# Expert loop of a routed mixture: row gather and scatter-add by DMA replaced by register-addressed column copies and adds on a transposed residual

## The chip, the cores and the metric

One core of a Trainium2 chip runs the whole program in one launch. The metric is device time in microseconds (us), the median of three runs: 1949.67 us before the change (1949.06 to 1951.79). All data is fp32.

## The reference

Two layers work on 640 tokens of width 1024: 128 context tokens and 512 latent tokens. Each layer does a modulated RMSNorm, one input projection, a convolution module beside differential attention, an output projection with a gated residual, and then a mixture of 16 experts. Each expert picks 80 tokens itself (16 context, 64 latent) by the top affinities, so a token can be picked by several experts or by none:

```python
aff = jax.nn.softmax(jnp.einsum('btd,de->bte', h, w_router).astype(jnp.float32), axis=-1)
gsel, idx = lax.top_k(aff.transpose(0, 2, 1), C)
xs = jax.vmap(lambda hb, ib: hb[ib])(h, idx)
hid = jax.nn.silu(jnp.einsum('becd,edf->becf', xs, w_gate)) * jnp.einsum('becd,edf->becf', xs, w_up)
ye = jnp.einsum('becf,efd->becd', hid, w_down) * gsel[..., None].astype(h.dtype)
return jax.vmap(lambda yb, ib: jnp.zeros((T, D), yb.dtype).at[ib.reshape(-1)].add(yb.reshape(-1, D)))(ye, idx)
...
x = x + g2 * expert_choice(h2, w_router, w_gate, w_up, w_down)
```

`h2` is the normed and modulated residual. A final RMSNorm of both token sets is the output.

## The kernel before

Weights stream through `weight_ring`, six slots of 2 MB. An expert has six units in order: gate (first half of the input features), up (first half), gate and up (second halves), down (two halves). SyncE issues the load of unit i of expert e as soon as unit i of expert e-1 has been used (`expert_used`), so the ring holds one whole expert and the order of the loads is fixed. Weights are the stationary operand; the 80 tokens of an expert are 80 moving columns, in two column groups of the array.

Before the loop, the router phase takes one token tile of 128 after another. For each it forms the residual `x2` (token rows in `x_tile`, stored to `x_res` in DRAM), squares it, gets 1/rms on GpSimd, scales the rows (`x_norm`), stores them to `x_unit` in DRAM, transposes them, modulates them (`h2_t`) and gets the router's logits. VectorE then finds the 8 largest of each expert ten times over (L1364 to L1369). The indices are transposed into `row_idx`, one expert per column.

In the loop, for expert e:

- GpSimd gathers 80 rows of `x_unit` by an indirect DMA (L1546), TensorE transposes them (L746) while expert e-1 is still at work, and VectorE scales and shifts them into `picked_t` (L1418, L1420).
- TensorE does gate and up (L760), ScalarE a SiLU of each half (L1031), VectorE the product (L1426), TensorE down (L777).
- ScalarE copies the result out of PSUM (L1039), TensorE transposes it back to token rows (L790), VectorE applies affinity and gate (L1433), and GpSimd adds the rows into `x_res` by an indirect DMA with addition (L1564).

The order on TensorE is gate and up of e, transposes of the picks of e+1, down of e, transposes of the result of e. It is written out by hand. TensorE, ScalarE and VectorE go round a real loop.

After the loop, all rows of `x_res` are loaded again (`x_all`), squared, scaled and transposed (L486) for the next layer's projection (L527), or squared and scaled for the output (L1456).

## Time and profile before

| | |
|---|---|
| runs of the kernel (3) | 1949.06, 1949.67, 1951.79 us; median 1949.67 |
| the profiled execution | span 1948.8 us from first to last instruction; no other time is given for it |
| mean granted clock of TensorE | 0.952 |
| TensorE matmuls busy | 1717.8 us (88%) |
| VectorE, ScalarE, GpSimd busy | 630.2, 327.0, 139.3 us |
| read from and written to DRAM | 509.30 and 24.64 MB |
| expert loop of layer 0, first gate matmul to last down matmul | 449.68 to 971.75 us |
| expert loop of layer 1 | 1396.28 to 1918.02 us |

The profile shows the busy share of each engine, the transfers, and for each idle time what ended it. A busy share says little about the bound: what counts in the loop is which wait of TensorE ends last. The clock is given as a share of 2.4 GHz, so 0.50 is the lower level of 1.2 GHz.

### The profile page before, as it was taken

To read this page: it belongs to the slowest core of one execution; us is meant where nothing else is said; L and a number is where in the kernel's file an instruction comes from. 1 tells how busy PE (TensorE), PEld (TensorE's weight loads), DVE (VectorE), ACT (ScalarE), POOL (GpSimd) and SP (SyncE) were. 2 spreads that over 40 slices of the span, in tenths; PEclk is the share of its full clock that TensorE was granted. 3 is DMA by queue.
4 is the path that set the end of the run, shared out by engine and by line. 5 is a ranking of instruction groups with operands and counts; after the bars stand their busy time and mean duration, and the time that the engine had idled before them with its cause. 6 is when DMAs were issued, how large, how long until landed. Compare 5 with 4: busy or idle time off the path is not lost.

```text
span 1948.8 us, 60484 instructions
## 1 busy us (share of the span) xinstructions
PE 1717.8 (88%) x28403; PEld 1357.9 (70%) x28403; DVE 630.2 (32%) x1056; ACT 327.0 (17%) x667; POOL 139.3 (7%) x169
## 2 busy tenths in 40 slices
PE   4999988967998899898969998899499999898983
PEld 2555456547998889888845444755489988898883
DVE  2399277251111111010127975832411111010112
ACT  3100156320010101010030003542110101010001
POOL 2100000100000000000010000000000000000002
PEclk9999999988999999999979999999699999999997
DMA  9246540436999999999941643033499999999995
GB/s 360 84 173 236 196 162 1 170 143 239 384 388 399 388 398 399 388 399 387 394 161 55 221 167 139 13 119 130 147 386 389 393 395 399 387 400 389 399 388 211
DMA packets 154439, 534.70 MB, mean 274 GB/s; under 512 B 5937, under 2 KB 6354, under 8 KB 154386
## 3 DMA queue, kind: packets, MB, share of 16 engines
q1 hardware_dynamic: 139600, 484.99, 64.6%
q0 software_dynamic: 12320, 42.47, 7.5%
q10 hardware_dynamic: 2466, 6.50, 0.8%
q8 instruction: 37, 0.61, 0.1%
q14 instruction: 16, 0.13, 0.0%
HBM read 509.30 MB, written 24.64 MB: 274 GB/s over the span
## 4 chain that ended last, share of the span: by engine, by line
PE 57%; DMA 30%; DVE 8%; SPq 2%; ACT 2%; issue 1%; POOL 0%; ACTq 0%; POOLq 0%; DVEq 0%
DMA weight_ring<-in_w_gate_dram 24%; PE ps L760 17%; PE ps L527 14%; PE ps L666 7%; PE ps L777 6%; PE ps L564 3%; DMA weight_ring<-in_w_down_dram 3%; PE ps L457 2%; DVE neg_m L1264 2%; SPq L356 2%; PE ps L626 1%; DMA weight_ring<-in_conv_w_dram 1%; PE ps L790 1%; DVE weight_ring L1300 1%; PE ps L686 1%
## 5 line engine op out<-in xcount | busy, mean ns | idle before, releaser
L760 PE MATMUL ps<-v_sb,weight_ring 128*64 128x80 f32 x16384 | 614.0, 238 | 74.9 <-DMA weight_ring<-in_w_gate_dram 51.4
L760 PEld LDWEIGHTS ps<-v_sb,weight_ring 128*64 128x64 f32 x16384 | 599.1, 141 | 93.0 <-DMA weight_ring<-in_w_gate_dram 54.7
L777 PE MATMUL ps<-mix,weight_ring 128*64 128x80 f32 x8192 | 294.3, 233 | 7.5 <-DMA weight_ring<-in_w_down_dram 4.3
L777 PEld LDWEIGHTS ps<-mix,weight_ring 128*64 128x64 f32 x8192 | 286.5, 137 | 14.5 <-issue 10.1
L527 PE MATMUL ps<-mix,weight_ring 128*128 128x512 f32 (+1 forms) x1024 | 285.1, 439 | 1.3 <-DVE mix L1158 1.0
L527 PEld LDWEIGHTS ps<-mix,weight_ring 128*128 128x128 f32 x1024 | 155.1, 193 | 130.1 <-issue 128.8
L1426 DVE TENSOR_TENSOR mix<-mix,ps 128x320 f32<-128x320 f32 x64 | 28.3, 483 | 644.5 <-PE ps L760 644.5
L1186 DVE SCALAR_TENSOR_TENSOR weight_ring<-u_gate,conv_cols,weight_ring 128x655 f32<-128x655 f32 x240 | 195.3, 887 | 0.0
L666 PE MATMUL ps<-weight_ring,mix 128*128 128x512 f32 x320 | 140.2, 592 | 0.0
L1433 DVE SCALAR_TENSOR_TENSOR qk<-ps,gsel,gate 80x1024 f32<-80x1024 f32 x32 | 41.0, 1280 | 284.7 <-PE ps L790 284.7
L1564 POOL DMA_INDIRECT x_res<-qk,row_idx x32 | 46.2, 1444 | 972.2 <-DVE qk L1433 941.2
L1031 ACT ACTIVATE mix<-ps 128x320 f32<-128x320 f32 x64 | 24.5, 435 | 536.6 <-PE ps L760 536.6
L666 PEld LDWEIGHTS ps<-weight_ring,mix 128*128 128x128 f32 x320 | 59.5, 190 | 67.9 <-issue 67.8
L1039 ACT ACTIVATE mix<-ps 128x320 f32<-128x320 f32 x64 | 28.0, 437 | 446.9 <-PE ps L777 446.9
L564 PE MATMUL ps<-weight_ring,mix 128*128 128x512 f32 x160 | 70.5, 595 | 0.0
L951 ACT ACTIVATE weight_ring<-ps,neg_m 128x640 f32<-128x640 f32 (+1 forms) x80 | 55.7, 706 | 5.1 <-DVE neg_m L1264 5.1
L1264 DVE TENSOR_REDUCE neg_m<-ps 128x2 f32<-128x1280 f32 (+1 forms) x40 | 50.8, 1273 | 15.6 <-PE ps L601 15.3
L564 PEld LDWEIGHTS ps<-weight_ring,mix 128*128 128x128 f32 x160 | 29.7, 190 | 36.4 <-issue 36.4
L457 PE MATMUL ps<-weight_ring,cond_silu 128*32 128x512 f32 x384 | 48.6, 629 | 0.8 <-issue 0.8
L612 PE MATMUL ps<-ident,weight_ring 128*128 128x128 f32 x168 | 32.4, 296 | 18.4 <-DVE o_tok L1283 9.0
L626 PE MATMUL ps<-v_sb,weight_ring 128*128 128x128 f32 x272 | 43.8, 303 | 4.9 <-ACT weight_ring L970 4.8
L626 PEld LDWEIGHTS ps<-v_sb,weight_ring 128*128 128x128 f32 x272 | 35.6, 202 | 10.9 <-ACT weight_ring L970 6.2
(183 smaller groups left out, 1178.0 us busy)
## 6 DMA issues: line engine op xcount, KB each, us to landing
weight_ring<-in_w_gate_dram SPq DMA_DIRECT2D x64, 2048.0 KB, 23.8
weight_ring<-in_w_up_dram SPq DMA_DIRECT2D x64, 2048.0 KB
weight_ring<-in_w_down_dram SPq DMA_DIRECT2D x64, 2048.0 KB, 26.5
weight_ring<-in_w_mod_dram SPq DMA_DIRECT2D x24, 2048.0 KB, 8.2
weight_ring<-in_w_in_dram SPq DMA_DIRECT2D x10, 2048.0 KB, 12.6
weight_ring<-in_w_out_dram SPq DMA_DIRECT2D x4, 2048.0 KB, 9.2
x_res<-x_tile POOLq DMA_DIRECT2D x10, 512.0 KB, 3.3
x_unit<-x_norm ACTq DMA_DIRECT2D x10, 512.0 KB, 2.6
```

Of the source, the lines that this page charges most:

```text
L457: last = nc.tensor.matmul(ps[c * STRIP:(c + 1) * STRIP, 6, :], cond_silu[:, k, at:at + STRIP], w[:, k, :], start=(k < 4 and g == 0), stop= ...
L527: last = nc.tensor.matmul(ps[:, 2 * (n % 3) + bank, 0:cols.stop - cols.start], w[:, k, tokens(b)], mix[:, k, cols], start=(at == 0), stop= ...
L564: last = nc.tensor.matmul(ps[:, 2 * (n % 3), :], mix[:, k, tokens(t)], w[:, k, :], start=(k == 0), stop=(k == KD - 1))
L626: last = nc.tensor.matmul(ps[:, 7, tokens(1)], a_col[:, tokens(j)], vals, start=(j == 0), stop=(j == n - 1))
L666: last = nc.tensor.matmul(ps[:, 2 * (i % 2) + n, :], mix[:, k, tokens(t)], w[:, k % 4, n * BANK:(n + 1) * BANK], start=(at == 0), stop=(at ...
L760: last = nc.tensor.matmul(ps[c * HALF:(c + 1) * HALF, 2 * (i % 2) + f // BLK, f % BLK * CAP:(f % BLK + 1) * CAP], w[:, kk, o:o + HALF], pi ...
L777: last = nc.tensor.matmul(ps[c * HALF:(c + 1) * HALF, 4 + d // BLK, d % BLK * CAP:(d % BLK + 1) * CAP], w[:, kk, o:o + HALF], hid[:, k, :] ...
L951: last = nc.scalar.activation(prob[:, b, m, 0:n], score_rows(s)[:, m, :], ACT.Exp, bias=neg_m[:, b, m:m + 1], accum_out=row_sum[:, b, m:m ...
L1186: ins = nc.vector.scalar_tensor_tensor(acc[:, j, :], src, w, acc[:, j, :], ALU.mult, ALU.add)
L1264: nc.vector.tensor_reduce(neg_m[:, s % 2, :], score_rows(s), AX, ALU.max, negate=True)\
L1433: nc.vector.scalar_tensor_tensor(added, ps[0:CAP, 6:8, :].rearrange("p b n -> p (b n)"), gsel[:, bass.ds(e, 1)], gate2[:], ALU.mult, ALU.m ...
L1564: nc.gpsimd.indirect_dma_start(out=x_res, out_offset=bass.IndirectOffsetOnAxis(ap=row_idx[:, e:e + 1], axis=0), in_=added, in_offset=None, ...
```

## The change

The normed and modulated tokens of all tiles stay on chip, transposed, in `mix`, and the residual stays on chip, transposed, in `x2_t` (features on partitions, one column per token in each of 8 blocks). A picked token is then one column in 8 blocks. Each pick is copied by one instruction whose address comes from a register: GpSimd copies picks 0 to 31 (`pick_lo`), ScalarE picks 32 to 79 (`pick_hi`). The result is added back in the same way: GpSimd adds picks 0 to 31, VectorE picks 32 to 79. The registers are loaded eight at a time. Gather, scatter-add, `x_unit`, `row_idx`, the transposes L746 and L790, the modulation L1418 and L1420 and the copies L1039 go. Affinity times gate is formed on VectorE once per expert (`gain_of`) and multiplied in on the way out of PSUM. In the router phase 1/rms is spread over the partitions by a small matmul. The indices and affinities of all experts go to DRAM and back once per layer. `picked_t` is one buffer, so the picks of e+1 wait for the end of gate and up of e. After the loop TensorE transposes the residual back from `x2_t`. The loops of ScalarE, VectorE and GpSimd are written out; that of TensorE stays a loop.

```diff
+PICK_SPLIT = 32
+PICK_LOAD = 8
...
+        def picks_of(engine, e, at, n):
+            src = top_i[0:1, at:at + n] if e == 0 else pick_row[:, e * CAP + at:e * CAP + at + n]
+            return nc.values_load_multi_w_load_instructions(
+                src, engines=[engine], min_val=0, max_val=(N_LAT if at < CAP_LAT else N_CTX) - 1,
...
+        def picked_row(j, pick):
+            rows = mix[:, :, N_CTX:N_TOK] if j < CAP_LAT else mix[:, :, 0:N_CTX]
+            return rows[:, :, bass.ds(pick, 1)]
...
 # TensorE, after and before the loop
+            def transpose_back(l, t):
+                if t == 0:
+                    pe.wait_ge(*added_lo.at(l - 1, EXPERTS))
+                    pe.wait_ge(*added_hi.at(l - 1, EXPERTS))
+                if t >= 3:
+                    pe.wait_ge(*(x_kept if l < DEPTH else y_ready).at(0, t - 2))
+                for k in range(KD):
+                    last = nc.tensor.transpose(ps[:, 2 * (t % 3) + k // 4, tokens(k % 4)], x2_t[:, k, tokens(t)], ident[:])
...
                 def gate_up(e):
-                    pe.wait_ge(*picked_ready.at(l, e + 1))
+                    pe.wait_ge(*picked_lo_ready.at(l, e + 1))
+                    pe.wait_ge(*picked_hi_ready.at(l, e + 1))
...
                     gate_up(e)
                     pe.wait_ge(*result_taken.at(l, e + 1))
-                    picked_transposes(e + 1)
                     down(e)
-                    result_transposes(e)
...
 # ScalarE
+                def pick_hi(e):
+                    for at in range(PICK_SPLIT, CAP, PICK_LOAD):
...
+                        for j, pick in enumerate(picks_of(mybir.EngineType.Activation, e, at, PICK_LOAD), at):
+                            last = nc.scalar.activation(picked_t[:, :, j:j + 1], picked_row(j, pick), ACT.Copy)
+                    last.then_inc(picked_hi_ready.sem, 1)
...
+                    if e + 1 < EXPERTS:
+                        act.wait_ge(*expert_used.at(l, e * 6 + 4))
+                        pick_hi(e + 1)
...
 # VectorE
+                def keep_x(t):
+                    dve.wait_ge(*x_transposed.at(l, t + 1))
+                    nc.vector.tensor_copy(x_stage[t], ps[:, 2 * (t % 3):2 * (t % 3) + 2, :].rearrange("p b n -> p (b n)"))\
...
+                def gain_of(e):
+                    nc.vector.tensor_tensor(result_gain, gate2_x[:],
+                                            gains[:, e, :].unsqueeze(1).to_broadcast([P, KD, CAP]), ALU.mult)\
...
                 def gated_result(e):
...
+                        last = nc.vector.tensor_tensor(result_t[:, cols, :], halves(4 + half), result_gain[:, cols, :],
+                                                       ALU.mult)
+                    last.then_inc(result_taken.sem, 1)
...
+                def add_hi(e):
+                    dve.wait_ge(*result_taken.at(l, e + 2))
+                    for at in range(PICK_SPLIT, CAP, PICK_LOAD):
+                        for j, pick in enumerate(picks_of(mybir.EngineType.DVE, e, at, PICK_LOAD), at):
+                            x = residual_row(j, pick)
+                            last = nc.vector.tensor_tensor(x, x, result_t[:, :, j:j + 1], ALU.add)
+                    last.then_inc(added_hi.sem, 1)
...
 # GpSimd
-                    nc.gpsimd.indirect_dma_start(
-                        out=x_res, out_offset=bass.IndirectOffsetOnAxis(ap=row_idx[:, e:e + 1], axis=0),
-                        in_=added, in_offset=None, compute_op=ALU.add)\
...
                 for e in range(EXPERTS):
+                    if e + 1 < EXPERTS:
+                        pool.wait_ge(*expert_used.at(l, e * 6 + 4))
+                        pick_lo(e + 1)
+                    add_lo(e)
```

Three places show the new order. The first is the body of TensorE's expert loop. Before:

```order
L760 MATMUL ps<-v_sb,weight_ring 64x80 [waits expert_loaded3]
L760 MATMUL ps<-v_sb,weight_ring 64x80 x63
L744 ISA [waits result_taken]
L746 MATMUL ps<-ident,qk 128x80 [waits gathered]
L746 MATMUL ps<-ident,qk 128x80 x7
L770 ISA [waits expert_loaded4]
L777 MATMUL ps<-mix,weight_ring 64x80 [waits hid_ready]
L777 MATMUL ps<-mix,weight_ring 64x80 x63
L770 REGISTER_ALU [waits expert_loaded5]
L777 MATMUL ps<-mix,weight_ring 64x80 [waits hid_ready]
L777 MATMUL ps<-mix,weight_ring 64x80 x63
L790 MATMUL ps<-ident,mix 80x128 [waits result_copied,picked_scaled]
```

The same place of the changed kernel, from the last gate and up unit to the top of the loop, where the next expert begins:

```order
L811 MATMUL ps<-v_sb,weight_ring 64x80 [waits expert_loaded3]
L811 MATMUL ps<-v_sb,weight_ring 64x80 x63
L821 ISA [waits expert_loaded4,result_taken]
L828 MATMUL ps<-v_sb,weight_ring 64x80 [waits hid_ready]
L828 MATMUL ps<-v_sb,weight_ring 64x80 x63
L821 REGISTER_ALU [waits expert_loaded5]
L828 MATMUL ps<-v_sb,weight_ring 64x80 [waits hid_ready]
L828 MATMUL ps<-v_sb,weight_ring 64x80 x63
L836 REGISTER_ALU
L836 COMPARE_AND_BRANCH
```

The transposes on either side of down are gone; the wait for the picks (`picked_hi_ready`, `picked_lo_ready`) stands at the top of the loop, behind down. The second place is ScalarE's body of the expert loop. Before:

```order
L1031 ACT_TABLE_LOAD
L1031 ACTIVATE mix<-ps 128x320 [waits expert_used] x2
L1036 REGISTER_ALU
L1039 ACTIVATE mix<-ps 128x320 [waits result_lo_done]
L1038 REGISTER_ALU
L1039 ACTIVATE mix<-ps 128x320 [waits expert_used]
```

In the changed kernel, the SiLUs of expert 0 and the beginning of the picks of expert 1:

```order
L1087 ACTIVATE v_sb<-ps 128x320 [waits expert_used]
L1089 ACTIVATE v_sb<-ps 128x320
L314 TENSOR_LOAD x_tile [waits picks_loaded,expert_used]
L1081 ISA
L1081 ACTIVATE v_sb<-mix 128x8
L1081 ISA
L1081 ACTIVATE v_sb<-mix 128x8
```

A TENSOR_LOAD fills eight registers, and an ISA (a register calculation of the address) stands ahead of each copy. There are six loads and 48 pairs for each expert. The third place is VectorE, after the result of expert 0 in the changed kernel:

```order
L1491 TENSOR_TENSOR u_gate<-ps,x_tile 128x320 [waits result_lo_done,result_gained]
L1491 TENSOR_TENSOR u_gate<-ps,x_tile 128x320 [waits expert_used]
L1468 TENSOR_TENSOR x_tile<-gate_x,u_gate 128x640 [waits result_taken]
L314 TENSOR_LOAD top_i [waits result_taken]
L1500 ISA
L1500 TENSOR_TENSOR qk<-qk,u_gate 128x8
L1500 ISA
L1500 TENSOR_TENSOR qk<-qk,u_gate 128x8
```

Before, one instruction of 80x1024 stood there (L1433) and the rest was the scatter's; now 48 pairs and six loads stand between the result and the next expert's product.

## Rows read from the trace of the kernel before

**Rows 1.** The page: its line of engines, and its chain that ended last.
```profile
PE 1717.8 (88%) x28403; PEld 1357.9 (70%) x28403; DVE 630.2 (32%) x1056; ACT 327.0 (17%) x667; POOL 139.3 (7%) x169
PE 57%; DMA 30%; DVE 8%; SPq 2%; ACT 2%; issue 1%; POOL 0%; ACTq 0%; POOLq 0%; DVEq 0%
```
**Rows 2.** Waits, 449.7 to 975 us: us in total, times, longest.
```profile
PE ps L760 <- DMA weight_ring<-in_w_gate_dram: 24.5, 10, 3.0
```
**Rows 3.** Transfers, 622 to 940 us: GB/s in 40 slices; packets, MB, share.
```profile
GB/s 408 410 384 367 411 410 403 349 410 408 411 345 407 411 411 370 382 411 410 380 373 409 408 395 362 408 410 411 342 410 411 408 343 410 408 411 363 387 411 410
q1 hardware_dynamic: 30107, 119.59, 95.3%
q0 software_dynamic: 1728, 5.90, 7.5%
```
**Rows 4.** Chain in order of time: start us, us, what; one undisturbed expert.
```profile
483.72 18.07 PE ps L760 x511
502.50 9.05 PE ps L777 x256
```
**Rows 5.** Timeline: start us, us, engine, line, operation; ends of both loops and what follows.
```profile
449.68 14.68 PE L760 MATMUL ps<-v_sb,weight_ring 128*64 128x80 f32 x377 [1.93 <-DVE v_sb L1420]
962.68 9.07 PE L777 MATMUL ps<-mix,weight_ring 128*64 128x80 f32 x256
971.69 1.24 PE L790 MATMUL ps<-ident,mix 128*80 128x128 f32 x8
999.23 4.17 PE L527 MATMUL ps<-mix,weight_ring 128*128 128x128 f32 x21
1396.28 17.10 PE L760 MATMUL ps<-v_sb,weight_ring 128*64 128x80 f32 x415 [1.92 <-DVE v_sb L1420]
1913.37 4.65 PE L777 MATMUL ps<-mix,weight_ring 128*64 128x80 f32 x128 [0.27 <-DMA weight_ring<-in_w_down_dram]
1939.73 1.28 DVE L1456 SCALAR_TENSOR_TENSOR qk<-qk,rstd,v_sb 128x1024 f32<-128x1024 f32 x1 [0.44 <-POOL rstd L1473]
```
**Rows 6.** Groups by line: busy us, mean ns of one, idle before; small instructions.
```profile
L917 ACT ACTIVATE lam_e<-lam_e 128x4 f32<-128x4 f32 x1 | 0.2, 205 | 0.0
L1369 DVE MATCH_VALUE_LOAD qk<-qk 16x8 f32 x16 | 0.9, 59 | 0.0
L1107 DVE TENSOR_TENSOR mod<-ps,par_cols 128x16 f32<-128x16 f32 x4 | 0.5, 164 | 0.0
L1475 POOL MEMSET eps<- 128x1 f32 x1 | 0.1, 98 | 0.3 <-POOLq L1604 0.3
L1031 ACT ACTIVATE mix<-ps 128x320 f32<-128x320 f32 x64 | 24.5, 435 | 536.6 <-PE ps L760 536.6
```
**Rows 7.** Timeline, as rows 5: two SiLUs in a row, and a GpSimd instruction.
```profile
653.24 0.77 ACT L1031 ACTIVATE mix<-ps 128x320 f32<-128x320 f32 x2 [15.36 <-PE ps L760]
386.21 0.56 POOL L1473 TENSOR_TENSOR rstd<-mean_sq,neg_half 128x1 f32<-128x1 f32 x1 [2.35 <-DVE mean_sq L1330]
```
**Rows 8.** Windows: us, busy PE, PEld, DVE, ACT, POOL; granted clock, DMA share, GB/s.
```profile
974.00:975.00 1.00, 0.00 (x0) 0.00 (x0) 0.44 (x1) 0.00 (x0) 0.00 (x0) 0.93 1.06 391
422.00:423.00 1.00, 0.00 (x0) 0.00 (x0) 1.00 (x3) 0.33 (x2) 0.02 (x1) 0.50 1.06 426
452.00:453.00 1.00, 1.00 (x26) 1.00 (x24) 0.00 (x0) 0.00 (x0) 0.00 (x0) 0.69 0.00 0
1396.00:1401.50 5.50, 5.22 (x78) 5.23 (x80) 0.15 (x1) 0.00 (x0) 0.00 (x0) 0.50 0.21 63
```
**Rows 9.** Timeline, as rows 5: TensorE before 422 us, and transposes at half clock.
```profile
415.99 1.88 PE L666 MATMUL ps<-weight_ring,mix 128*128 128x512 f32 x4
987.72 1.97 PE L486 MATMUL ps<-ident,qk 128*128 128x128 f32 x8 [14.78 <-DVE qk L1124]
```
**Rows 10.** Groups by line, as rows 6: what a tile costs between the layers.
```profile
L1323 DVE TENSOR_TENSOR conv_tmp<-ps,u_gate 128x1024 f32<-128x1024 f32 x10 | 12.2, 1224 | 88.8 <-PE ps L666 88.8
L1158 DVE TENSOR_SCALAR mix<-mix,scale,mod 128x128 f32<-128x128 f32 x4 | 1.4, 341 | 0.0
```

More of the change, by code:

```diff
@@ L1551, in _, with pick_lo @@
-                pool.wait_ge(*result_taken.at(l, 1))
-                pool.wait_ge(*unit_stored.at(l, TILES))
-                gather(0)
+                def pick_lo(e):
+                    for at in range(0, PICK_SPLIT, PICK_LOAD):
+                        if e == 0:
+                            pool.wait_ge(*top_round.at(l, at // 8 + 1))
+                        elif e == 1 and at == 0:
+                            pool.wait_ge(*picks_loaded.at(l, 1))
+                        for j, pick in enumerate(picks_of(mybir.EngineType.Pool, e, at, PICK_LOAD), at):
+                            last = nc.gpsimd.tensor_copy(picked_t[:, :, j:j + 1], picked_row(j, pick))
+                    last.then_inc(picked_lo_ready.sem, 1)
@@ new lines, in add_lo @@
+                def add_lo(e):
+                    pool.wait_ge(*result_taken.at(l, e + 2))
+                    if e > 0:
+                        pool.wait_ge(*added_lo.at(l, e))
+                        pool.wait_ge(*added_hi.at(l, e))
+                    for at in range(0, PICK_SPLIT, PICK_LOAD):
+                        for j, pick in enumerate(picks_of(mybir.EngineType.Pool, e, at, PICK_LOAD), at):
+                            x = residual_row(j, pick)
+                            last = nc.gpsimd.tensor_tensor(x, x, result_t[:, :, j:j + 1], ALU.add)
+                    last.then_inc(added_lo.sem, 1)
```

389 lines of the change are left out of this document (197 added, 192 removed).

## The prediction

> **What bounds the kernel now.** I read the page first. TensorE is busy 88% of the span, and the chain that ended last gives it 57% and transfers 30% [rows 1]; a share of 30% that is all one kind of wait means a second limit in some stage. The chain in order of time then shows where: two long stretches, one expert loop per layer, from 449.68 to 971.75 us (962.68 + 9.07) and from 1396.28 to 1918.02 us (1913.37 + 4.65), 522.1 and 521.7 us, together 54% of the span [rows 5]. In the first loop TensorE waits for gate weights ten times, 24.5 us in all, never over 3.0 us at once [rows 2]. Between 622 and 940 us the queue of the weights fills 95.3% and the software queue (gather and scatter) 7.5% of all transfer engines: full [rows 3]. 119.59 MB at 12.58 MB an expert (six units of 2 MB) are 9.5 experts in 318 us, 33.4 us each. Yet TensorE itself needs only 18.07 us for gate and up and 9.05 us for down [rows 4]: 27.1 us. So in the loop the transfers are the bound, with TensorE 6 us behind them, less its two groups of transposes (one of them 1.24 us [rows 5]). At the start of each loop TensorE is the bound, because one expert is already loaded.
>
> **What goes.** Gather and scatter leave the transfer engines. In slices that carry weights almost alone the rate is 410 to 411 GB/s, against 342 to 384 in those with gathers [rows 3]; at 410.5 GB/s 12.58 MB take 30.65 us. The transfers would allow 33.4 - 30.65 = 2.75 us less per expert, 15 intervals of a loop 41 us, two loops 82 us. That is all the change can win in the loops, and it needs TensorE to come round in 30.65 us, that is, with at most 30.65 - 18.07 = 12.6 us between the end of gate and up of e and the start of those of e+1. Down fills 9.05 of them.
>
> **What comes: the picks.** Before, the picks of e+1 were fetched a whole expert ahead, into another buffer. Now they are copied into the one `picked_t`, so they start when gate and up of e end, and TensorE cannot go on before both engines are done. ScalarE's part is six loads of eight registers and 48 pairs of an address calculation and a copy of 8 columns. The trace shows none of the three, so each is bounded by neighbours.
>
> - A copy: the nearest row is an ACTIVATE of 4 elements on chip, 205 ns [rows 6]. Two of 320 columns in a row take 0.77 us, where one takes 435 ns [rows 7, 6]: the second starts 100 ns before the first ends. So 0.105 us per copy in a row.
> - The address calculation: nearest is VectorE's small MATCH_VALUE_LOAD, 59 ns [rows 6]; I take 0.06 us. A pair is then 0.165 us. Ends: 0.10 us (the calculation hidden behind the copy) and 0.30 us (205 ns unoverlapped and a calculation of 100 ns).
> - A load of eight registers: each register a small read of its own between 59 and 205 ns [rows 6]; middle 0.13 us, so 1.06 us for eight. Ends: 0.2 us (all eight as one such read) and 1.64 us (8 x 205 ns).
>
> ScalarE: 6 x 1.06 + 48 x 0.165 + 0.1 for the handing over = 14.4 us. Ends: 6.1 us and 24.3 us. GpSimd: 4 loads and 32 pairs. Its smallest instruction is 98 ns (a memset), and a two-input one of a single column 0.56 us [rows 6, 7]; with the middle, 0.33 us, 4 x 1.06 + 32 x 0.33 = 14.8 us, with the ends 3.9 and 24.5 us. Both engines thus come out near 14.4 us, which I take, and both ends belong to the range.
>
> 14.4 us against the 12.6 us allowed: TensorE, not the transfers, becomes the bound in every expert, with an idle gap of 14.4 - 9.05 = 5.35 us.
>
> Here a sentence of the Trainium skill speaks against the change (Runtime: NRT & Kernel Launch, Instruction fetch mechanics): a register load costs about 200 ns for each register, even in bulk, because each is a round trip. It is said of loads from DRAM, and no run here shows one. By it a load of eight is 1.6 us, the picks 9.6 + 7.9 + 0.1 = 17.6 us and the sum below 96 us higher, an estimate.
>
> **The clock.** After TensorE's last matmul at 417.87 us (415.99 + 1.88) the granted clock is 0.50 by 422 us; after 972.93 us (971.69 + 1.24) it has begun to fall by 975 us, 0.93 in the slice before [rows 9, 5, 8]. So after 2 to 4 us with nothing to do the engine is put from 2.4 to 1.2 GHz. The 3.0 us waits of the loop stay just short of it or lose little; a gap of 5.35 us does not. The way back: at the start of the loops the clock is 0.50 from 449.68 to about 452.7 us (0.69 in that slice) and from 1396.28 to 1401.5 us [rows 5, 8]. Work of 3.0 and 5.2 us at half speed loses 1.5 and 2.6 us; I take 2.0 us per expert, ends 0 and 2.6.
>
> **The loop's sum.** 16 x 18.07 + 9.05 + 15 x (14.4 + 2.0) = 544.2 us, and 2.0 us for the slow first start, which both kernels have: 546.2 us. Against 522.1 and 521.7 us this is +24.1 and +24.5, together +48.6 us.
>
> The adds stay beside. VectorE has 6 x 1.06 + 48 x 0.19 = 15.5 us (a 128x16 sum takes 164 ns [rows 6], and some spacing) behind the result and `gain_of` (0.5 + 0.8 us), and the next product is wanted 18.07 + 5.35 + 2 us after the end of down: 16.8 of 25.4 us. What is queued behind the last add is that product, and TensorE's down waits for it; if the adds took over 23 us this cover would be gone. GpSimd's adds, like its copies 14.8 us, lie between two of its picks with 20 us for them. Of what goes, L746 and L790 are in the sum, since it counts only 18.07 and 9.05 us of TensorE; ScalarE's table loads and copies (L1039), L1418, L1420 and L1433 were beside the weights and count nothing.
>
> **Between the loops.** Before, 27.5 us from the end of down (971.75) to the first projection matmul (999.23) [rows 5]. Now: the result's second half 0.5 us, the last adds 15.5 us with nothing to hide them, 1.97 us for eight transposes at half clock [rows 9], 1.2 us for a square. Then VectorE does for each of five tiles a copy out of PSUM and a mean (1.22 + 0.15 us), and for the four that the first matmul waits for a product (1.22 us) and four modulations of 0.34 us [rows 10]: 5 x 1.4 + 4 x 2.65 = 17.6 us. Sum 36.8 us, +9.3, and about 0.7 us more before the fifth tile: +10 us. What goes is the scatter's landing and the reload of `x_res`; what is late next is VectorE.
>
> **At the end.** Before, 30.8 us from 1918.02 us to the span's end, the last 7.8 us of them after VectorE's last row (1939.73 + 1.28) [rows 5]. Now 16.1 us for result and adds, 2 us of transposes, 1.2 us square, 1 us for mean and root, five tiles at the 1.45 us of VectorE, 1.5 us for the reuse of PSUM: 29 us, and 7.8: +6 us. Ends for both places together: -5 (adds 5 us) and +45.
>
> **The router phase** I cost at nothing. VectorE has one more product per tile, ScalarE a copy in place of a scaling; the projection L666 hides four tiles of five, and the fifth (+1.2 us on VectorE) is paid by the gather and the transposes that no longer stand behind the last maximum. ScalarE must catch up with 15 us of picks of expert 0, though, so I book no gain; ends -6 and +6 us per layer. The round trip of the indices through DRAM is needed only for expert 1, 18 us later.
>
> **Sum.** 48.6 + 10 + 6 = +64.6 us on the profiled 1948.8 us: 2013 us, and as the median of the runs lies 0.9 us above that span, 2014 us.
>
> **Rivals.** (1) The picks fit: faster. If loads cost near 0.5 us and pairs near 0.12 us the picks take 9 us, down hides them, and TensorE does 27.2 us within the 30.65 us of the transfers. Then -82 + 16 (both tails, with shorter adds perhaps 10): 1949.7 - 82 + 16 = 1884 us. It decides itself at 12.3 us: (522 - 298 - 2)/15 = 14.8 us per gap is even with no clock loss, 12.8 with it, and the tails' 16 us take another 0.5 off. For it: the lower bounds are wide open, and the sequencer may run ahead of the engine. Against: six loads one after another in a 9 us window. (2) GpSimd is the bound: at its own 0.56 us for each of its 64 instructions and 8 loads of 1.06 us it needs 44 us per expert, and 15 x (44.3 - 34.5) x 2 = 294 us more: about 2300 us. For: its 0.56 us row; against: that row computes a power. (3) The picks take 12 to 13 us, gain and loss cancel: 1950 us. (4) Picks at 17 to 19 us by dearer registers: 2014 + 30 x 3.2 = 2110 and more. (5) That the traffic does not fall at all has little for it: 5.90 MB of the software queue in 318 us are exactly the gathered and added rows.
>
> **Chances.** Forecast (1960 to 2110 us) 0.46; (1) 0.32; (3) 0.08, half of it within 0.2%; (4) and (2) together 0.14. A measurement of this kernel tells about 0.2% (4 us) from no change. Faster: 0.32 + 0.03 = 0.35; same 0.04; slower 0.61. The range for 8 in 10 takes in most of rival (1) and the beginning of (4): 1875 to 2125 us. If the forecast's own mechanism holds, 1975 to 2090 us.
>
> **What would show it.** Right: in the loop TensorE waits at the top of each expert for ScalarE's or GpSimd's copies, 5 us each time, no longer for gate weights; the granted clock in the loops is visibly below 0.98; the rate of the transfers falls to about 12.58 MB in 36 us, 350 GB/s; the last adds stand bare before both reloads' successors. Wrong: waits for gate weights of 1 to 3 us remain and the rate stands at 410 GB/s (rival 1), or TensorE waits for GpSimd alone and ScalarE is long done (rival 2), or TENSOR_LOADs well below 0.5 us.

## The result, and the profile after

The changed kernel takes 1880.26 us, median of four runs (1879.4 to 1883.72), against 1949.37 us for the kernel before in the same session (1948.44 to 1951.79): ratio 0.9644, 95% interval 0.9623 to 0.9664, so 3.6% faster. The forecast was 2014 us and slower; its rival (1), the picks fit, had 1884 us. The profiled execution took 1879.4 us with a span of 1877.6 us; the rows below are from it. Of all executions below one, in experiment 4, ran at a granted clock of 0.818 and took 2080.51 us where the nine others had 0.945 to 0.953, and its ratio leaves that one out.

| | before | after |
|---|---|---|
| span of the profiled execution | 1948.8 us | 1877.6 us |
| mean granted clock | 0.952 | 0.963 |
| TensorE, VectorE, ScalarE, GpSimd busy | 1717.8, 630.2, 327.0, 139.3 us | 1652.2, 816.4, 446.3, 374.0 us |
| software queue (gather, scatter, small loads) | 42.47 MB | 10.36 MB |
| expert loop of layer 0, of layer 1 | 522.1, 521.7 us | 488.3, 488.5 us |
| last down matmul of layer 0 to first projection matmul | 27.5 us | 34.3 us |
| last down matmul of layer 1 to the span's end | 30.8 us | 27.0 us |

The differences add up: loops -33.8 and -33.2, the stretch before the first loop -2.4, between the layers +6.8, from there to the second loop -4.9, the end -3.8, together -71.3 us of the 71.2 us between the spans. The loops are nearly all of it. The two stretches ahead of the loops (-2.4 and -4.9) are not shown to be the change's: the first loop begins at 447.32 us here and at 444.71 us in another execution of the same instructions (the first of the five runs in experiment 5), and from the first projection matmul to the second loop experiment 1, which changes nothing there, took 397.7 us, the changed kernel 392.2 and the kernel before 397.1.

First the page after, its engines and its queues over the whole span (packets, MB, share of 16 engines):

```profile
PE 1652.2 (88%) x27925; PEld 1304.6 (69%) x27925; DVE 816.4 (43%) x2587; ACT 446.3 (24%) x2105; POOL 374.0 (20%) x2131
...
q1 hardware_dynamic: 140740, 488.95, 67.0%
q0 software_dynamic: 3104, 10.36, 1.6%
...
q14 instruction: 102, 0.84, 0.1%
```

Three engines work more than before, and the kernel is faster; the waits below show that their added work is covered in the loops. Now the transfers in the stretch of the second loop that the weights pace, 1506 to 1790 us, which answers to [rows 3]:

```profile
GB/s 410 410 407 410 409 409 410 408 411 406 410 410 409 409 408 410 409 410 406 411 408 409 411 407 412 407 410 410 407 411 407 411 407 410 410 405 405 411 410 407
DMA packets 29209, 116.13 MB, mean 409 GB/s; under 512 B 884, under 2 KB 884, under 8 KB 29183
...
q1 hardware_dynamic: 29183, 115.92, 102.3%
q14 instruction: 26, 0.21, 0.2%
```

The dips to 342 to 384 GB/s of [rows 3] are gone: no slice is under 405, the mean is 409 GB/s, on weights alone. One thing is new: a queue that loads instructions, about three packets of 8 KB per expert. It comes back in the experiments.

Next the waits of TensorE in the second loop (us in total, times, longest), for [rows 2]. L811 is gate and up, L828 down, L1081 ScalarE's copies of the picks and L1476 VectorE's product:

```profile
PE ps L811 <- DMA weight_ring<-in_w_up_dram: 13.5, 21, 1.4
PE ps L811 <- DMA weight_ring<-in_w_gate_dram: 12.6, 21, 1.4
PE ps L828 <- DVE v_sb L1476: 9.5, 15, 0.7
PE ps L811 <- ACT v_sb L1081: 7.8, 1, 7.8
```

TensorE waited for ScalarE's picks once, ahead of expert 0; in experts 1 to 15 never. The forecast wanted 5 us there each time. What it waits for instead is weights, in the units' own rhythm of some 5.1 us. One expert of this stretch on TensorE's timeline:

```profile
1599.20 4.65 PE L811 MATMUL ps<-v_sb,weight_ring 128*64 128x80 f32 x128 [0.39 <-DMA weight_ring<-in_w_gate_dram]
1604.32 4.65 PE L811 MATMUL ps<-v_sb,weight_ring 128*64 128x80 f32 x128 [0.47 <-DMA weight_ring<-in_w_up_dram]
1610.40 4.65 PE L811 MATMUL ps<-v_sb,weight_ring 128*64 128x80 f32 x128 [1.43 <-DMA weight_ring<-in_w_gate_dram]
1615.53 4.65 PE L811 MATMUL ps<-v_sb,weight_ring 128*64 128x80 f32 x128 [0.48 <-DMA weight_ring<-in_w_up_dram]
1620.84 4.65 PE L828 MATMUL ps<-v_sb,weight_ring 128*64 128x80 f32 x128 [0.66 <-DVE v_sb L1476]
1625.85 4.65 PE L828 MATMUL ps<-v_sb,weight_ring 128*64 128x80 f32 x128 [0.36 <-DMA weight_ring<-in_w_down_dram]
1630.88 4.65 PE L811 MATMUL ps<-v_sb,weight_ring 128*64 128x80 f32 x128 [0.39 <-DMA weight_ring<-in_w_gate_dram]
```

Gate and up end at 1620.18 us, down ends at 1630.50 us. Between the two, ScalarE's picks of the next expert (the same stretch of its timeline, groups of eight copies):

```profile
1620.90 0.97 ACT L1081 ACTIVATE v_sb<-mix 128x8 f32 x8 [5.03 <-PE ps L811]
1622.33 0.96 ACT L1081 ACTIVATE v_sb<-mix 128x8 f32 x8 [0.47 <-issue]
...
1628.27 0.95 ACT L1081 ACTIVATE v_sb<-mix 128x8 f32 x8 [0.68 <-issue]
```

The first copy stands 0.7 us behind gate and up, a group comes every 1.45 us, and the last ends at 1629.22 us: 9.0 us, 1.3 us ahead of the end of down. GpSimd's four groups ended at 1626.73 us. The prices by themselves (durations in ns: least, median, most; then first and last start in us; the address calculation is FUSED_REGOPS):

```profile
L314 POOLq TENSOR_LOAD <-x_tile x240: 562/563/602, 469.0 to 1856.1; - x120
L314 ACTq TENSOR_LOAD <-x_tile x180: 537/546/583, 469.0 to 1816.2; - x180
L314 DVEq TENSOR_LOAD <-x_tile x180: 593/595/628, 507.8 to 1859.8; - x180
L1081 ACTq FUSED_REGOPS  x1536: 37/46/57, 437.4 to 1817.4; - x192
L1081 ACT ACTIVATE v_sb<-mix x1536: 198/203/222, 437.5 to 1817.8; 128x8 f32 x192
```

Eight copies take 0.96 us, 0.12 us each with one copy's full length of 203 ns at the end, so they start 0.108 us apart, and the calculation of 46 ns lies beneath. A load costs mostly 0.47 us of gap (once 0.68 in this expert), not its 546 ns.

Last the stretch between the layers, which answers to rows of [rows 5]:

```profile
936.94 1.14 DVE L1500 TENSOR_TENSOR qk<-qk,u_gate 128x8 f32 x8 [0.78 <-DVE u_gate L1491]
...
946.67 5.35 PE L521 MATMUL ps<-ident,qk 128*128 128x128 f32 x24 [11.04 <-DVE qk L1500]
...
969.93 30.34 PE L583 MATMUL ps<-mix,weight_ring 128*128 128x128 f32 x114 [3.15 <-DVE mix L1194]
```

TensorE waits 11 us for the last adds, then the five tiles go through VectorE one by one.

### The profile page after: what moved, and what is told of

Read it like the earlier page. It is cut to its first block and busy times, and to the rows that moved or that the text cites. A ratio compares the mean times of both kernels' runs of the same rounds, so it can differ in the third digit from the quotient of the medians.

```text
span 1877.6 us, 69913 instructions
## 1 busy us (share of the span) xinstructions
PE 1652.2 (88%) x27925; PEld 1304.6 (69%) x27925; DVE 816.4 (43%) x2587; ACT 446.3 (24%) x2105; POOL 374.0 (20%) x2131
## 3 DMA queue, kind: packets, MB, share of 16 engines
q0 software_dynamic: 3104, 10.36, 1.6%
## 5 line engine op out<-in xcount | busy, mean ns | idle before, releaser
L811 PE MATMUL ps<-v_sb,weight_ring 128*64 128x80 f32 x16384 | 592.0, 234 | 72.1 <-DMA weight_ring<-in_w_up_dram 27.1
L811 PEld LDWEIGHTS ps<-v_sb,weight_ring 128*64 128x64 f32 x16384 | 576.1, 138 | 87.8 <-DMA weight_ring<-in_w_up_dram 33.8
L828 PE MATMUL ps<-v_sb,weight_ring 128*64 128x80 f32 x8192 | 296.0, 233 | 32.9 <-DVE v_sb L1476 18.9
L828 PEld LDWEIGHTS ps<-v_sb,weight_ring 128*64 128x64 f32 x8192 | 287.0, 137 | 41.8 <-DVE v_sb L1476 26.4
L1500 DVE TENSOR_TENSOR qk<-qk,u_gate 128x8 f32 x1536 | 210.1, 190 | 96.4 <-issue 94.9
L1081 ACT ACTIVATE v_sb<-mix 128x8 f32 x1536 | 187.3, 205 | 233.6 <-PE ps L811 152.8
L1621 POOL COPY v_sb<-mix 128x8 f32 x1024 | 143.6, 200 | 490.9 <-PE ps L811 434.2
L1632 POOL TENSOR_TENSOR qk<-qk,u_gate 128x8 f32 x1024 | 184.5, 220 | 210.4 <-DVE u_gate L1491 197.5
L1476 DVE TENSOR_TENSOR v_sb<-v_sb,ps 128x320 f32<-128x320 f32 x64 | 28.4, 484 | 315.5 <-PE ps L811 315.5
L1491 DVE TENSOR_TENSOR u_gate<-ps,x_tile 128x320 f32<-128x320 f32 x64 | 31.5, 492 | 284.7 <-PE ps L828 284.7
L1087 ACT ACTIVATE v_sb<-ps 128x320 f32<-128x320 f32 x32 | 14.0, 438 | 519.8 <-PE ps L811 519.8
L1323 DVE TENSOR_REDUCE neg_m<-ps 128x2 f32<-128x1280 f32 (+1 forms) x40 | 50.8, 1274 | 16.0 <-PE ps L657 15.5
## 6 DMA issues: line engine op xcount, KB each, us to landing
weight_ring<-in_w_in_dram SPq DMA_DIRECT2D x10, 2048.0 KB, 12.6
```

Source lines behind the costliest of these rows:

```text
L811: last = nc.tensor.matmul(ps[c * HALF:(c + 1) * HALF, 2 * (i % 2) + f // BLK, f % BLK * CAP:(f % BLK + 1) * CAP], w[:, kk, o:o + HALF], pi ...
L828: last = nc.tensor.matmul(ps[c * HALF:(c + 1) * HALF, 4 + d // BLK, d % BLK * CAP:(d % BLK + 1) * CAP], w[:, kk, o:o + HALF], hid[:, k, :] ...
L1081: last = nc.scalar.activation(picked_t[:, :, j:j + 1], picked_row(j, pick), ACT.Copy)
L1323: nc.vector.tensor_reduce(neg_m[:, s % 2, :], score_rows(s), AX, ALU.max, negate=True)\
L1500: last = nc.vector.tensor_tensor(x, x, result_t[:, :, j:j + 1], ALU.add)
L1621: last = nc.gpsimd.tensor_copy(picked_t[:, :, j:j + 1], picked_row(j, pick))
```

## The experiments

Theory 1: the gain is transfer time, opened by gather and scatter leaving full transfer engines, and the picks cost nothing as long as they fit between gate and up of one expert and the next. Rivals: TensorE's shorter program made the gain (theory 2); the picks are already at the edge. The time between the starts of successive experts is called their distance below; it is the mean over the last nine of a loop, for layer 0 and layer 1, where nothing else is said. Every ratio is to the kernel before, timed beside the run.

### 1. ScalarE's picks doubled

```diff
                             last = nc.scalar.activation(picked_t[:, :, j:j + 1], picked_row(j, pick), ACT.Copy)
+                        if e > 0:
+                            for j, pick in enumerate(picks_of(mybir.EngineType.Activation, e, at, PICK_LOAD), at):
+                                last = nc.scalar.activation(spare[:, :, j:j + 1], picked_row(j, pick), ACT.Copy)
```

> The changed kernel with ScalarE doing each group of picks twice from expert 1 on: the second time into a spare buffer. Six more loads and 48 more copies per expert, which is the length of picks that the forecast had feared. In the trace after the change a group of eight takes 1.45 us and the first starts 0.7 us after gate and up, so twelve groups end 18.1 us after gate and up. Theory 1 (picks are a window problem: nothing under down plus slack, everything beyond it): TensorE becomes the bound, 18.07 + 18.1 + 0.4 = 36.6 us an expert where it was 31 on average; the loop takes 16 x 18.07 + 9.05 + 15 x 18.5 = 576 us against 488, in total 1880 + 176 = 2056 us; if the idle gap of 9 us also drops the clock as the forecast had it (2.0 us each), 2116 us. Rival (TensorE does not depend on the length of the picks, since the transfers set the pace with some larger reserve): 1880 to 1900 us.

Measured: 2098.72 us, ratio 1.0756 (1.0723 to 1.0788). TensorE's timeline (L1086 is the second copy, into the spare buffer):

```profile
1572.73 9.07 PE L828 MATMUL ps<-v_sb,weight_ring 128*64 128x80 f32 x256 [0.59 <-DVE v_sb L1481]
1589.88 19.98 PE L811 MATMUL ps<-v_sb,weight_ring 128*64 128x80 f32 x512 [8.07 <-ACT conv_tmp L1086]
1610.44 9.07 PE L828 MATMUL ps<-v_sb,weight_ring 128*64 128x80 f32 x256 [0.59 <-DVE v_sb L1481]
1627.81 19.79 PE L811 MATMUL ps<-v_sb,weight_ring 128*64 128x80 f32 x512 [8.29 <-ACT conv_tmp L1086]
```

This is the picture that the forecast drew: TensorE waits 8 us for picks at the top of each expert, and gate and up take 19.8 to 20.0 us where they take 17.93 at full clock, 1.9 to 2.0 us lost to the clock (granted 0.50 from 1589.9 to 1593.0 us). The distance is 37.5 us, the loops 595.6 and 595.8 us. Gate and up end at 1609.86 us and the last copy at 1627.57 us, 17.7 us later. The forecast's own sum with these 17.7 us and its 2.0 us for the clock, 16 x 18.07 + 9.05 + 15 x 19.7 + 2, is 595.7 us. So where picks outlast the window its mechanism holds, and so does its clock term at this wait; in the loop only the length of the picks was wrong.

### 2. More picks on ScalarE: the edge of the window

```diff
-PICK_SPLIT = 32
+PICK_SPLIT = 16
```

> The changed kernel with PICK_SPLIT 16 instead of 32: ScalarE copies 64 picks of an expert, GpSimd 16, VectorE adds 64. Theory 1: ScalarE's eight groups of 1.45 us end 0.7 + 11.6 = 12.3 us after gate and up, TensorE could go round in 18.07 + 12.3 + 0.4 = 30.8 us, still inside the 31 us that the weights take: no change in the loops, 488 us each, and only VectorE's last adds are 3.3 us longer at two places: 1887 us. If an idle gap of 3.2 us already costs TensorE its clock, up to 2.0 us in each expert on top, the loops grow by up to 30 us each and the total is up to 1945 us. Rival (picks were already at the edge of the window, any microsecond more counts in full): 3 us in each of 30 experts, 1970 us.

Measured: 1898.64 us, ratio 0.9737 (0.9705 to 0.977); span 1892.0 us.

```profile
1587.22 17.93 PE L811 MATMUL ps<-v_sb,weight_ring 128*64 128x80 f32 x512 [2.46 <-ACT v_sb L1081]
1605.73 9.07 PE L828 MATMUL ps<-v_sb,weight_ring 128*64 128x80 f32 x256 [0.58 <-DVE v_sb L1476]
1617.25 19.37 PE L811 MATMUL ps<-v_sb,weight_ring 128*64 128x80 f32 x512 [2.45 <-ACT v_sb L1081]
```

TensorE now waits 2.5 us for picks in each expert, and weights are always there: the picks are the bound, but only just. The distance alternates between 30.05 and 31.6 us, as the clock after the wait holds (17.93 us, granted 1.00 throughout) or falls (19.37 us, granted 0.68 from 1617.2 to 1622.0 us). Its mean, 30.8 us, is even below the 31.5 us of the changed kernel; the loops are 493.2 and 491.2 us all the same (+4.9, +2.7), because the four distances of 27.5 us early in each loop are now 30 us and more too. The rival at the edge (1970 us) falls. The picks end so that TensorE starts 12.1 us after gate and up, just inside the 12.6 us that the forecast allowed, and there the gain starts to shrink. Its even point of 12.3 us is not borne out: at 12.1 us the loops are still 28.9 and 30.5 us shorter than before, because a wait of 2.5 us cost nothing or 1.4 us of clock and not the 2.0 us that the forecast charged at every length.

### 3. The kernel before without the rows' traffic

This kernel leaves out the scatter-adds and the gathers from expert 2 on, so its results are wrong; only its time is used.

```diff
-                    nc.gpsimd.indirect_dma_start(
-                        out=x_res, out_offset=bass.IndirectOffsetOnAxis(ap=row_idx[:, e:e + 1], axis=0),
-                        in_=added, in_offset=None, compute_op=ALU.add)\
+                    pool.dma_start(x_res[0:1, 0:16], added[0:1, 0:16])\
                       .then_inc(residual_written[0].sem, 16)
```

and the same for the gathers from expert 2 on.

> The kernel before with gathers from expert 2 on and all scatter-adds replaced by software-queue transfers of 64 bytes in the same places: order, waits, transposes and modulation of the kernel before stay; each row past the first gathers is stale and nothing is added to the residual. Theory 1 (the gain of the change is that gather and scatter leave the transfer engines): the experts come 30.7 us apart instead of 33.4, both loops lose up to 41 us: 1870 us, at least 50 us under 1949. Theory 2 (the gain comes from TensorE's sixteen transposes per expert and the waits around them): nothing changes here, 1949 us. In between, say 1910 us, would mean both.

Measured: 1863.13 us, ratio 0.9556 (0.9525 to 0.9588). The loops are 480.9 and 480.4 us, 41.2 and 41.3 us shorter, where the forecast had 41 us as the most that the transfers can give. The distance is 28.9 us while TensorE sets the pace (27.1 us and its two groups of transposes) and 30.7 us after that. Theory 2 falls: with all its transposes the old program reaches the transfers' pace. The shorter program shows only where TensorE sets the pace (27.5 us against 28.9). But this also shows that the changed kernel, 488.4 us a loop, leaves 8 us of each loop on the table.

### 4. The traffic put back

```diff
+                    pool.dma_start(conv_tmp_flat[0:CAP, 0:D], x_sample[0, 0:CAP, :]).then_inc(extra.sem, 16)
+                    pool.dma_start(scratch, mix_flat[0:CAP, 0:D]).then_inc(extra.sem, 16)
                     add_lo(e)
```

> The changed kernel with two more transfers on GpSimd's software queue in each expert, 80 rows of 4 KB from DRAM into a spare buffer and 80 rows of 4 KB from on-chip memory to a scratch tensor: the bytes of a gather and a scatter, 0.66 MB, with nothing that waits for them in the loop. Theory 1 (the gain came from transfer time): at 409 GB/s 0.66 MB are 1.6 us, by the spacing of experts before (33.4 against 30.7) 2.7 us; in the ten or so experts of a loop that the weights pace, that is +16 to +27 us per loop, so 1912 to 1934 us; if the whole loop pays, up to 1960 us. Rival (TensorE's shorter program made the gain): 1880 us stays.

Measured: 1955.97 us over ten executions, 1954.35 us over the nine beside the long one, ratio of these 1.001 (0.9989 to 1.0032): the whole gain is gone, near the upper end of what was expected (32 to 80 us more). In each loop TensorE still waits for picks only once, ahead of expert 0; its added waits are for weights. The distance is 33.9 and 33.6 us, that of the kernel before (33.6 and 33.6), the loops 525.0 and 525.3 us. The transfers of this kernel from 1506 to 1790 us:

```profile
q1 hardware_dynamic: 27338, 108.58, 96.7%
q0 software_dynamic: 1551, 5.31, 5.7%
q14 instruction: 23, 0.19, 0.2%
```

5% more bytes (0.66 MB on 12.58) cost 2.2 us of 31.5, 7% more time; by their bytes at 409 GB/s it would be 1.6 us. And more than ten experts of a loop paid: at the slower pace the lead of the loaded expert is used up after three experts instead of five, and experts 4 to 6 came 10 us later in sum. Together with experiment 3, theory 1 holds from both sides.

### 5. Where 8 us of each loop went: code that is loaded in the loop

In the stretch above 12.58 MB at 409 GB/s are 30.75 us, but experts come up to 31.67 us apart: once per expert one wait for weights is 1.43 us instead of 0.47. The kernel before had next to no instruction packets there, the changed one three per expert.

```diff
-                for e in range(EXPERTS):
-                    gated_hidden(e)
-                    gated_result(e)
-                    if e + 1 < EXPERTS:
-                        gain_of(e + 1)
-                    add_hi(e)
+                dve_expert(0)
+                with dve.Fori(1, EXPERTS - 1) as e:
+                    dve_expert(e)
+                dve_expert(EXPERTS - 1, False)
```

and the same on ScalarE and GpSimd.

> The changed kernel with the expert loops of ScalarE, VectorE and GpSimd as real loops (first and last expert written out). Reason: in the stretch where the weights set the pace the transfer engines move 409 GB/s, which is 30.75 us for 12.58 MB, yet experts come 31.66 us apart. In that stretch the instruction queue moves about 3 packets of 8 KB per expert. If all go over one of the 16 engines, that one has 786 + 24.6 KB to carry instead of 786, 3.1% or 0.96 us more, and the slowest engine sets when a unit has landed. Theory: with real loops the code is fetched once, the instruction packets vanish from the loop and the experts come 30.75 us apart: -0.9 us in about 10 experts of each loop, 1862 us. Rival a (the 0.96 us come from the back edge of SyncE's or TensorE's loop): no change, 1880 us. Rival b (address arithmetic and back edges make picks or products later): slower than 1880 us.

Measured: 1859.72 us, ratio 0.9547 (0.9509 to 0.9585); expected 1862. The distance is 30.72 us, to 0.02 us the same in all of the last nine experts; the loops are 479.3 and 478.4 us. From 1506 to 1790 us there is no instruction packet:

```profile
q1 hardware_dynamic: 29287, 116.33, 102.6%
```

```profile
1610.20 4.65 PE L814 MATMUL ps<-v_sb,weight_ring 128*64 128x80 f32 x128 [0.39 <-DMA weight_ring<-in_w_gate_dram]
1615.33 4.65 PE L814 MATMUL ps<-v_sb,weight_ring 128*64 128x80 f32 x128 [0.48 <-DMA weight_ring<-in_w_up_dram]
1620.44 4.65 PE L814 MATMUL ps<-v_sb,weight_ring 128*64 128x80 f32 x128 [0.47 <-DMA weight_ring<-in_w_gate_dram]
1625.57 4.65 PE L814 MATMUL ps<-v_sb,weight_ring 128*64 128x80 f32 x128 [0.47 <-DMA weight_ring<-in_w_up_dram]
...
1640.92 4.65 PE L814 MATMUL ps<-v_sb,weight_ring 128*64 128x80 f32 x128 [0.40 <-DMA weight_ring<-in_w_gate_dram]
```

Three waits of 0.4 to 0.5 us in a row, and none of 1.43 us is left. How much code costs how much was asked in five more runs. The first of them added 128 empty instructions on two engines:

> The changed kernel with 128 empty instructions behind each expert's adds on VectorE and 128 on GpSimd, nothing moved besides: 16.4 KB more code per expert. Theory (the code of unrolled loops comes over one of the 16 transfer engines, and the slowest engine sets when weights land): 2 more packets per expert on that one, 16.4 KB of 786 KB, 2.1% or 0.64 us on top of the 0.96 us seen, so experts 32.3 us apart, +0.64 us in 10 to 15 experts of each loop: 1893 to 1899 us, and the instruction queue shows 5 packets per expert. Rival (the code is hidden, the 0.96 us have another cause that the real loops happened to remove): 1880 us.

Measured: 1879.78 us, ratio 0.9622 (0.9593 to 0.9651), but the trace has 69913 instructions and 102 instruction packets, exactly as the changed kernel: the empty ones are not in it, and this was one more timing of the changed kernel. Small real operations instead:

```diff
+                        for i in range(256 + e % 2 * 96, 352 + e % 2 * 96):
+                            nc.scalar.activation(conv_tmp_flat[:, i:i + 1], ones[:, 0:1], ACT.Copy)
```

and 64 memsets on VectorE, 48 on GpSimd.

> The changed kernel with small independent operations behind each expert's work, which nothing waits for: 64 one-column memsets on VectorE (about 4 us), 48 on GpSimd (about 5 us), 96 one-column copies on ScalarE (about 10 us, behind its picks, so its next SiLU is still in time at 31 us an expert). 208 instructions of 64 bytes are 13.3 KB, 1.6 packets of 8 KB more per expert. Theory (code over one transfer engine sets the landing of the weights): 13.3 of 786 KB, 1.7% or 0.52 us, experts 32.2 us apart in the stretch that the weights pace, 10 to 13 experts of each loop: +10 to +14 us, 1890 to 1894 us, and the instruction queue shows about 4.4 packets per expert instead of 2.8. Rival (code costs nothing): 1880 us.

Measured: 1896.56 us, ratio 0.973 (0.9699 to 0.9761); distance 31.97 and 32.08 us; 39 instruction packets in nine experts, and TensorE's added waits are for weights (those for up in the first loop 20.8 us against 13.5). Then less code, by a real loop on GpSimd alone:

> The changed kernel with a real loop on GpSimd alone; ScalarE and VectorE stay written out. GpSimd has about 136 of the roughly 350 instructions of an expert on these three engines. Theory: 1.7 packets per expert remain of 2.8, the slowest transfer engine has 786 + 14 KB, experts 31.3 us apart, so a good third of the gain of the version with three real loops: 1880 - 0.37 x 20.5 = 1872 to 1873 us. Rival (the gain of the real loops sat in ScalarE's or VectorE's chain, not in the amount of code): 1880 us here.

Measured: 1879.11 us, ratio 0.9641 (0.9608 to 0.9673). 15 packets in nine experts instead of 25, and the distance as before, 31.59 and 31.45 us: a miss. Two runs on what that means, with real loops on ScalarE and VectorE, and on ScalarE alone:

> The changed kernel with real loops on ScalarE and VectorE, GpSimd written out: the complement of the run with a real loop on GpSimd alone, which still had 1.6 code packets per expert and experts 31.5 us apart over the last nine, no less than with all 2.7. Two readings of that. A: GpSimd's code costs nothing, ScalarE's and VectorE's costs 0.5 us per packet (0.85 us for 1.6 packets; 1.36 us for 2.9 in the run with more code). Then experts are 30.72 us apart here, as with three real loops: 1860 us. B: the delay comes in steps of 0.96 us and one step is due for any amount of code between about 1 and 3 packets. Then GpSimd's 1.1 packets give 31.5 us again: 1879 us. By bytes alone (the theory as first stated) it would be 31.07 us and 1868 us.

> The changed kernel with a real loop on ScalarE alone: 1.9 code packets per expert remain, 0.85 of them VectorE's, 1.1 GpSimd's. Reading A (GpSimd's free, 0.5 us per packet of the others): 30.72 + 0.43 = 31.15 us apart, 1869 us. Reading B (one step of 0.96 us in most experts): 31.5 us, 1879 us. By bytes alone 31.4 us, 1875 us.

Measured: 1874.85 us, ratio 0.9602 (0.958 to 0.9624), and 1881.31 us, ratio 0.9635 (0.9605 to 0.9665). All of them together:

| instruction packets in nine experts (layer 0; layer 1 has at most one fewer) | distance, layer 0 and 1 | run |
|---|---|---|
| 0 | 30.72, 30.72 us | real loops on three engines |
| 10 | 31.44, 31.44 | on ScalarE and VectorE |
| 15 | 31.59, 31.45 | on GpSimd |
| 18 | 31.57, 31.50 | on ScalarE |
| 25 | 31.57, 31.43 | the changed kernel |
| 39 | 31.97, 32.08 | more code |

So code that is loaded in the loop delays the weights, and reading A (GpSimd's is free) falls. But it is not by bytes: ten packets already cost 0.7 us an expert, 25 hardly more. Nor is there one step. In the changed kernel experts come 30.7 or 31.67 us apart, 0.96 us between the two; with real loops on ScalarE and VectorE, which leaves about one packet in each expert, nearly all come 31.36 to 31.38 us apart, 0.65 us over 30.72, while the packet itself takes 0.32 us. That all packets go over one transfer engine would explain the size of the changed kernel's delay and not this shape; it was only argued. How a packet comes to cost what it does stays open.

The Trainium skill (Runtime: NRT & Kernel Launch, Instruction fetch mechanics) calls the cost of streaming code in "mostly hidden", says that a taken branch stalls if its target is not in the two pages of code that are held, and has kernels prefer full unrolling where possible. Here the three unrolled loops cost 0.7 to 0.9 us per expert, so the trace does not agree on the first. The real loops (114, 124 and 150 instructions a round on ScalarE, VectorE and GpSimd) ran their later experts without one instruction packet, so no branch there had to fetch its target, and cost nothing that shows.

### 6. What a load of registers costs

```diff
-PICK_LOAD = 8
+PICK_LOAD = 4
```

> The changed kernel with four registers per load instead of eight: 20 loads per expert and role instead of 10, the same copies and adds. It prices the load. If a load costs by its registers, a load of four takes 0.27 us and the picks stay at 9.0 us; if it has a fixed part, each load stays near 0.5 us and ScalarE's picks grow by 6 x 0.5 = 3 us to 12 us. Either way they end at or before 12.3 us after gate and up, so the loops stay at 488 us with at most some clock loss, and only VectorE's last adds, up to 3 us longer twice, show: 1880 to 1890 us. The forecast's price of 0.13 us per register would be wrong in either case.

Measured: 1885.89 us, ratio 0.9642 (0.961 to 0.9674). The loads of four:

```profile
L314 POOLq TENSOR_LOAD <-x_tile x480: 313/318/354, 469.2 to 1866.5; - x160
L314 ACTq TENSOR_LOAD <-x_tile x360: 302/305/330, 469.2 to 1825.8; - x180
L314 DVEq TENSOR_LOAD <-x_tile x360: 335/342/364, 511.3 to 1870.2; - x180
```

305 ns for four and 546 ns for eight on ScalarE are 60 ns a register and 65 ns once. A group of four comes every 0.765 us, so twelve take 9.2 us where six of eight take 8.7: the number of loads hardly counts. The distances (31.6 and 31.7 us) and the ratio are those of the changed kernel.

### 7. A version that beats both

Real loops on three engines, and two pieces moved that nothing covers: the last eight picks of expert 0 go to GpSimd, which is idle there, and the last expert's adds are split 40 to 40.

```diff
-                    for at in range(PICK_SPLIT, CAP, PICK_LOAD):
+                    for at in range(PICK_SPLIT, CAP - (8 if isinstance(e, int) and e == 0 else 0), PICK_LOAD):
...
-                    for at in range(PICK_SPLIT, CAP, PICK_LOAD):
+                    for at in range(40 if isinstance(e, int) and e == EXPERTS - 1 else PICK_SPLIT, CAP, PICK_LOAD):
```

> The kernel with real loops on ScalarE, VectorE and GpSimd, and two pieces moved: the last eight picks of expert 0 are copied by GpSimd, which is idle there, instead of ScalarE (its last group ends 1.4 us after the one before, and TensorE waits for it at the start of each loop), and the last expert's adds are split 40 to 40 instead of 32 to 48 (GpSimd five groups of 1.6 us, VectorE five of 1.66 us: 8.3 us instead of 10 to 11). Nothing covers either piece, so both count in full: 2 x 1.4 + 2 x 1.9 = 6.6 us under the version with real loops, 1853 us. If another chain is just behind them (SyncE's round trip of the indices, VectorE's transposes) less: 1857 us.

Measured: 1853.71 us, ratio 0.9489 (0.9466 to 0.9512), 5.1% under the kernel before. Its waits:

```profile
PE ps L524 <- POOL qk L1645: 18.5, 2, 9.3
...
PE ps L814 <- POOL v_sb L1634: 14.1, 2, 7.1
```

Against the version with real loops alone the wait for the last adds fell from 21.8 to 18.5 us and that for the first picks from 15.9 to 14.1 us, 5.1 us of the 6.6 expected; the spans are 1851.8 and 1846.9 us. The intervals of the two runs' ratios overlap, so only the traces show this last step.

## Why the prediction was wrong

The measured 1880.26 us lies inside the range for 8 in 10 (1875 to 2125 us) only because that range took in rival (1); it is outside the 1975 to 2090 us of the forecast's own mechanism, and the direction was wrong.

**What bounds the kernel: right.** The forecast allowed the transfers 41 us per loop; experiment 3 gave 41.2 and 41.3.

**The picks: the step that failed.** "6 x 1.06 + 48 x 0.165 + 0.1 for the handing over = 14.4 us" measured 9.0 us. The load was sized at 1.06 us and takes 0.47 to 0.55 (six of them: 3 us too many); a pair was sized at 0.165 us and takes 0.12, since the 0.06 us booked for the address calculation lie under the copy ahead (2 us too many). The spacing of copies, 0.105 us from two SiLUs in a row, was right (0.108). The lower ends, 0.2 and 0.10 us, were nearer than the values taken. GpSimd was to need 14.8 us and needed 6.6. With 9.0 us the forecast's own rule, 12.6 us allowed, says that the picks are hidden; then both the gap of 5.35 us and the 2.0 us of clock behind it fall away in each of the 30 gaps. The clock alone was 60 of the +64.6 us. The chances did follow the range: of 6.1 to 24.3 us a share of 0.36 lies under 12.6, and faster had 0.35. What misled was the middle value of two terms for which no row existed: the load, taken as eight small reads one behind the other, and the address calculation, taken as standing between the copies.

**The register rule.** The forecast read the 200 ns per register of the Trainium skill (Runtime: NRT & Kernel Launch, Instruction fetch mechanics) as a price of loads from DRAM; the Trainium skill names no memory there, only "uncached AXI". It is no measure for these loads from on-chip memory: 60 ns a register, by experiment 6. It spoke for the wrong side here, and the estimate of +96 us with it.

**The clock term: plausible, but never called.** 2.0 us were booked for a gap of 5 us; experiment 1 shows 1.9 to 2.0 us at a gap of 8 us, experiment 2 none or 1.4 us at 2.5 us, and no run has a gap of 5 us. In the changed kernel the loop's granted clock is 1.00.

**The tails: too dear.** The last adds measured 10.4 us (forecast 15.5, the same two prices). Between the layers it was +6.8 us against +10; at the end -3.8 against +6. Between the layers the transposes and tiles behind them took 23.3 us against the forecast's 21.5. At the end, the 7.8 us after VectorE's last row [rows 5] were taken over into the sum unchanged and are 3.2 us now (the last two rows, one profile line, start at 1871.97 us and take 2.47). In the kernel before the last transfer was done at 1943.3 us, but GpSimd's closing DRAIN took 10.43 us and ended at 1948.6; in the changed kernel it takes 3.29 us and ends ahead of the last transfer.

**The router phase**, costed at nothing: the stretches that hold it are 2.4 and 4.9 us shorter. As shown above, executions of the same instructions differ as much, so no gain of the router phase is shown.

**Not in the forecast:** the product `hid` (L1476) stands bare between gate and up and down, since the transposes that covered it are gone, 0.6 us per expert; it costs only where TensorE sets the pace. And the code of the unrolled loops, 8 to 9.5 us per loop (488.4 us, against 480.6 in experiment 3 and 478.9 in experiment 5).

**The rival's number** was 1949.7 - 82 + 16 = 1884 us, 4 us high: the loops gave 67 us instead of 82, the tails cost 3 instead of 16, and the stretches ahead of the loops were 7 us shorter instead of none. Its number is near by luck, through errors that cancel; its mechanism is right.

## What to carry to other kernels

Where weights fill the transfer engines, work that takes bytes off them is worth its bytes and more (5% of the bytes were 7 to 9% of the time: 2.2 us put back, 2.9 us taken out, for 1.6 by bytes), and small work on three otherwise idle engines is free, but for its code, as long as it fits a window whose edge can be read from the trace. Name the edge first; if the new cost is pieced together from rows of other instructions and its range reaches across the edge, the sign of the change is open until that cost has a row of its own. Small register-addressed copies in a row cost their spacing, not their length plus their address calculation. And count what unrolled code adds where the transfer engines are full: real loops on all three engines gave back 20 us here, on ScalarE or on GpSimd alone nothing.

## What was not expected of the hardware

- A load of eight registers from on-chip memory takes 546 ns on ScalarE, 563 on GpSimd, 595 on VectorE; of four 305, 318 and 342 ns.
- Copies of 128x8 with register addresses start 0.108 us apart on ScalarE (203 ns long each); their address calculation of 46 ns shows nowhere. A group of eight takes GpSimd 1.12 us, and eight of its two-input adds 1.45 us (forecast 0.33 us for each pair, measured 0.14 and 0.18).
- Instruction packets of 8 KB (0.32 us each) in a stretch of full transfer engines go with weights that come later, and not in proportion to their bytes: 0.7 us per expert at ten packets in nine experts, 0.7 to 0.9 us at 15 to 25, 1.2 to 1.4 us at 39.
- After a wait of 2.46 us TensorE went on at full clock, after one of 2.45 us it lost 1.4 us: after waits of this length the granted clock held in some experts and fell in others.
- GpSimd's closing DRAIN took 10.43 us in the kernel before and 10.55 and 8.51 us in experiments 3 and 4, which all issue transfers on the software queue throughout the loops; in the changed kernel it took 3.29 us.
